# Attention units: the products with the values of one unit back ahead of the current unit's transposes

## The reference

```python
def masked_softmax(logits, mask):
    logits = jnp.where(mask, logits, -jnp.inf)
    m = jnp.max(logits, axis=-1, keepdims=True)
    p = jnp.exp(logits - m)
    return p / jnp.maximum(jnp.sum(p, axis=-1, keepdims=True), 1e-30)

# eight heads: o = g0 * o_cmp + g1 * o_slc + g2 * o_win
p = masked_softmax(jnp.einsum('bghqd,bgkd->bghqk', q_b, k_b) * scale, mask)
...
# four stick-breaking heads
z = jnp.einsum('bhqd,bhkd->bhqk', q_b, kf) * scale
log_1m = jnp.where(strict, log_beta - z, 0.0)
excl = lax.cumsum(log_1m, axis=3, reverse=True) - log_1m
a = jnp.where(strict, jnp.exp(log_beta + excl), 0.0)
...
# four forgetting heads: logits + c[query] - c[key], then masked_softmax
# memory: four heads, softmax over all 256 memory tokens
```

## Time and profile before

| | before |
|---|---|
| median of 3 runs | 1633.99 us (1633.25 to 1635.56) |
| the profiled execution's own time | 1634.43 us |
| its span | 1632.7 us |
| TensorE busy | 1587.6 us (97%) |
| VectorE busy | 1167.6 us (72%) |
| ScalarE busy | 816.3 us (50%) |
| GpSimd busy | 83.5 us (5%) |
| DMA | 293.67 MB, mean 180 GB/s |
| mean granted TensorE clock | 0.997 of full speed |

### The profile page before, as it was taken

How to read it: one execution, slowest core, us unless ns; L and a number is a source line. 1 busy time by engine, 2 the same in 40 slices (tenths; PEclk the granted TensorE clock), 3 DMA queues, 4 the chain that set the end, 5 groups by cost and what they waited for, 6 DMA issues and landing times.

```text
span 1632.7 us, 35998 instructions
## 1 busy us (share of the span) xinstructions
PE 1587.6 (97%) x12358; PEld 1474.2 (90%) x12358; DVE 1167.6 (72%) x1780; ACT 816.3 (50%) x1343; POOL 83.5 (5%) x89
## 2 busy tenths in 40 slices
PE   8999899999999989999999999999999999999998
PEld 7987789999897879999989888889999999999997
DVE  5774789988987478888867454568777678676744
ACT  5555666653456576654545222235555355555533
POOL 3000001110400000110000000000000000000000
PEclk9999999999999999999999999999999999999999
DMA  8440435458764135447925543348555765455551
GB/s 343 169 143 11 158 130 177 170 192 278 268 225 151 56 118 177 167 168 270 344 93 181 168 155 129 130 161 315 192 182 180 250 222 184 168 180 180 181 185 46
DMA packets 81164, 293.67 MB, mean 180 GB/s; under 512 B 9152, under 2 KB 10688, under 8 KB 80320
## 3 DMA queue, kind: packets, MB, share of 16 engines
q1 hardware_dynamic: 78912, 283.31, 49.8%
q10 hardware_dynamic: 2176, 9.31, 1.5%
HBM read 291.53 MB, written 1.05 MB: 179 GB/s over the span
## 4 chain that ended last, share of the span: by engine, by line
PE 73%; DVE 14%; ACT 6%; issue 4%; DVEq 1%; ACTq 1%; DMA 0%; POOL 0%; SPq 0%; POOLq 0%
PE projs L1632 34%; PE accs L1632 33%; PE ob L1632 5%; DVE WL L951 4%; ACT WH L472 3%; DVE mk L1314 2%; DVE cv L1323 2%; DVE cv L1321 1%; ACT FH L536 1%; DVE rstd L1082 1%; PE projs L1878 1%; DVE ring L968 1%; ACT scr L642 1%; DVE prod L1330 0%; DVE scr L1158 0%
## 5 line engine op out<-in xcount | busy, mean ns | idle before, releaser
L951 DVE TENSOR_TENSOR WL<-ring,WH 128x1024 fp32r<-128x1024 f32 x427 | 531.5, 1246 | 269.5 <-ACT WH L472 267.9
L472 ACT ACTIVATE WH<-ring 128x1024 fp32r (+1 forms) x419 | 441.6, 1057 | 545.2 <-PE projs L1632 270.5
L1632 PE MATMUL projs<-AH,WH 128*128 128x256 f32 (+2 forms) x2120 | 539.9, 292 | 12.3 <-ACT WH L472 4.1
L1632 PE MATMUL projs<-AL,WH 128*128 128x256 f32 (+2 forms) x2120 | 530.9, 287 | 0.3
L1632 PEld LDWEIGHTS projs<-AH,WH 128*128 128x128 f32 x2120 | 399.4, 189 | 28.8 <-DVE mk L1314 14.1
L1632 PEld LDWEIGHTS projs<-AL,WH 128*128 128x128 f32 x2120 | 401.2, 190 | 5.6 <-DVE AL L1109 1.7
L1632 PE MATMUL projs<-AH,WL 128*128 128x256 f32 (+2 forms) x2192 | 315.2, 285 | 0.4 <-DVE WL L951 0.4
L1632 PEld LDWEIGHTS projs<-AH,WL 128*128 128x128 f32 x2192 | 285.3, 189 | 7.6 <-DVE WL L951 3.1
L1632 PE MATMUL accs<-FH,WH 128*128 (+1 forms) x768 | 190.7, 285 | 2.0 <-ACT WH L472 2.0
L1632 PE MATMUL accs<-FL,WH 128*128 (+1 forms) x768 | 189.6, 279 | 0.0
L1632 PEld LDWEIGHTS accs<-FH,WH 128*128 128x128 f32 x768 | 144.0, 187 | 3.3 <-issue 3.3
(11 more groups left out here) (264 smaller groups left out, 1887.5 us busy)
## 6 DMA issues: line engine op xcount, KB each, us to landing
ring<-in_stream SPq DMA_DIRECT2D x532, 512.0 KB, 3.4
W1v<-in_w ACTq DMA_DIRECT2D x2, 1024.0 KB, 7.4
W1k<-in_w ACTq DMA_DIRECT2D x2, 1024.0 KB, 10.5
D<-in_decay ACTq DMA_DIRECT2D x4, 512.0 KB, 5.4
x<-in_xT SPq DMA_DIRECT2D x2, 512.0 KB, 4.9
memT<-in_memT SPq DMA_DIRECT2D x1, 1024.0 KB, 11.2
ctxT<-in_ctxT ACTq DMA_DIRECT2D x1, 1024.0 KB, 9.0
out_y<-ybuf SPq DMA_DIRECT2D x8, 128.0 KB, 2.0
```

Source lines behind the costliest of these rows:

```text
L472: A(WH[:, s, :], ring[:, r % RING, :], ACT.Copy).then_inc(wh_ready, 1)
L951: V.tensor_tensor(WL[:, s, :], ring[:, r % RING, :], WH[:, s, :].bitcast(F32), ALU.subtract).then_inc(consumed, 1)
L1632: return T.matmul(out, lhsT, rhs, start=start, stop=stop, skip_group_check=True)
```

## The change

In the loop over the units, TensorE issues `values(v - 1)` ahead of `turn(v)` instead of behind it. The other engines' streams are the same, row by row.

```diff
--- before.py
+++ after.py
@@ -1906,9 +1906,9 @@
                 for v in range(U):
                     if v + 2 < U:
                         scores(v + 2)
-                    turn(v)
                     if v:
                         values(v - 1)
+                    turn(v)
                 values(U - 1)
                 n["u"] += U
                 n["soft"] = softs[-1]
```

## The result

| | before | changed |
|---|---|---|
| median (6 runs each) | 1633.62 us (1632.96 to 1635.56) | 1640.36 us (1640.17 to 1640.60) |
| the profiled execution's own time | 1634.43 us | 1640.17 us |
| its span | 1632.7 us | 1638.5 us |
| TensorE busy | 1587.6 us | 1588.3 us |
| mean granted TensorE clock | 0.997 | 0.997 |

The account below looks back on a forecast made before the run. TensorE's own work, 73% of the span, was taken as the bound. Memory units 2.68, stick units +0.63 and -0.54, soft units 0 gave +2.77 us: 1637.20 for the profiled execution, 1636.8 for the median; range 1634.9 to 1639.2.

Parts of the forecast that it names:

- TensorE's scores run ahead by about 1.0 us by unit 7: Soft and forget units: values fill old waits, gaining 0.6 at turn(1) and some 0.2 each at turn(3) and turn(5).
- The copy of unit 8 starts at 539.68, not 539.65: Layer 1, soft units: the lead is spent again, unit 10's activations keep their time; 0 per layer, gain 0.9 to loss 0.4.
- or if turn(10) itself moves: Sign that the forecast is wrong: the start of stick unit 10's turn was expected to stay in place.
- Stick units: Layer 1: values(9) fits the idle gap, but turn(11) must wait for unit 10's copy and values(10): +0.63 us.
- I take -0.54: Layer 0's stick units: values(9) fills the idle stretch, the clock holds and turn(11) comes 0.54 us earlier; +0.55 if it falls.
- 1.61 us: Layer 0's stick units: cost given to the clock's fall, from turn(10) 3.27 against 2.18 and values(9) 1.32 against 0.80.
- rival (a): Nothing won back in layer 0: the clock falls there also, or usually did not before; 3.86 us, 1637.9, chance 0.28.
- turn(1) comes at 596.33: Memory units: turn(1) waits for the first copy and values(0), +1.34 us in each layer, 2.68 in all; bounds 1.2 and 1.5.
- Rival (b): The clock falls in the memory units because of TensorE's new idle times there: 1.6 us more, 1638.4, chance 0.12.

Follow-up runs that it names:

- units 1 to 7 alone: Kernel before with the new order in iterations 1 to 7 only, the old one from 8 on: 1636.28 us against 1634.33, ratio 1.0011.
- unit 8 alone: Kernel before with the new order in iteration 8 only, values(7) ahead of turn(8): 1635.80 us against 1634.33, ratio 1.0011.
- unit 11 alone: Kernel before with the new order in iteration 11 only, values(10) ahead of turn(11): 1635.95 us, ratio 1.0014.
- filled kernel: Changed kernel with four matmuls of a constant ahead of each values of the memory units: 1640.50 us against 1634.28 for the kernel before, ratio 1.0037.
- unit 10 alone: Kernel before with the new order in iteration 10 only, values(9) ahead of turn(10): 1633.14 us against 1634.28; repeated, 1633.68 against 1634.65.

## Why the prediction was wrong

Forecast for the profiled execution was +2.77 us; it became +5.74, and +6.74 between the medians. By the steps of the prediction:

1. **"TensorE's scores run ahead by about 1.0 us by unit 7": failed.** The first 0.6, at turn(1), came (scores(4) 0.62 earlier). The 0.2 each at turn(3) and turn(5) were eaten as they came: the lead of scores(5) to scores(8) is 0.47, 0.51, 0.35 and 0.39, then it shrinks to 0.25 at scores(9) and to 0.05 at scores(10). The reason lies in TensorE's own stream. Two iterations without a compressed product, with no wait in them, TensorE's timeline; before (v = 6):

```profile
530.20 0.38 PE L1632 MATMUL accs<-mqkb,identb 128*128 128x128 bf16 x4
530.42 0.82 PE L1878 MATMUL projs<-const,scr 128*128 128x128 f32 x6
531.17 0.87 PE L1632 MATMUL ob<-PT,Vt 128*64 128x256 f32 x8
531.97 0.71 PE L1632 MATMUL accs<-P 64*128 64x128 f32 x6
```

and the changed kernel (v = 2; its v = 6 takes 1.92):

```profile
518.04 0.40 PE L1632 MATMUL accs<-mqkb,identb 128*128 128x128 bf16 x4
518.37 0.87 PE L1632 MATMUL ob<-PT,Vt 128*64 128x256 f32 x8
519.17 0.88 PE L1878 MATMUL projs<-const,scr 128*128 128x128 f32 x6
519.97 0.71 PE L1632 MATMUL accs<-P 64*128 64x128 f32 x6
```

   From the mask to the next scores it is 1.77 us before and 1.93 now, with the same instructions: 0.16 more for the order. I had charged no price for an order of matmuls; several units of it eat the lead. Why the hand-overs cost more in this order (0.33 instead of 0.22 behind the mask, 0.80 instead of 0.75 behind the transposes) was not tried.

2. **"The copy of unit 8 starts at 539.68, not 539.65": failed.** In the same count it started about 0.75 later (543.51 - 507.30 = 36.21, before 539.65 - 504.19 = 35.46). So my own sign of being wrong came, "or if turn(10) itself moves". The delay follows from step 1 and from something that I overlooked. I followed turn(7), its copy, values(7) and turn(8), and left out that ScalarE does exps(9) between the copies of units 7 and 8. The run with units 1 to 7 alone shows this way by itself (0.37 in layer 1), the run with unit 8 alone the other (0.56). Together they cost 0.65 and 0.81 us at turn(10), where I had put 0 with an upper bound of 0.4 per layer. This is 1.46 of the 2.97 us that my sum lacked.

3. **Stick units, "+0.63": right.** Measured 0.62 in layer 1, and 0.61 with unit 11 alone. The move at unit 10 costs nothing, as forecast.

4. **"I take -0.54" for layer 0: the number came (0.55), the reason did not hold.** The fall was absent in this execution, but values(9) in the gap does not exclude it: it came in 5 of 16 layers with it. The "1.61 us" that I gave as the cost of the fall was also misread: it is how much longer turn(10) and values(9) took, but in layer 1 turn(11) had to wait 0.37 us for its cut behind them, so that the fall cost 4.59 - 3.42 = 1.17. The page of the Trainium skill that I had set against this step ("TensorE: Matmul & The Clock Gate", "What's actually happening") says that what watches the engine's activity is not reset when a kernel starts, so that the point of a change varies. The three traces of the changed kernel agree: beside the fall at the start that all of them have, they have one at 205, at 147 and at 550 us. I had given that possibility, rival (a), 0.28, and put only 1637.9 on it.

5. **Memory units, "turn(1) comes at 596.33", 2 x 1.34: right in mechanism, small by 0.15 each.** I took the starts of the values' pairs as the price of what follows them (4 x 0.215 = 0.86). The transposes behind them start only after 1.01 us, and so does their first weight load (the row at 600.85, with 0.39 us of idle PEld, "issue", ahead of it). Some 0.05 of the 0.15 could have been read before: the last of the eight starts 0.70 behind the first in both kernels (before, values(1): 597.29 to 597.99), and 0.215 more makes 0.91. The other 0.1 is the same error as in step 1: a hand-over between two kinds of matmuls that no row of before showed in this order. Why it takes longer is not shown. The whole makes 0.30 over both layers, and 1.5 was my upper bound.

6. **Rival (b) happened in this execution**: a fall behind the memory units, +1.52 (priced 1.6). Its reason stays open. One of eight such places had it in the new order and none of fourteen in the old, which is too little to say that the short waits bring it, and the filled kernel, without them, had its fall elsewhere. The same page of the Trainium skill ("A second HAM failure mode: psum-queue depth-cycling") would have the clock swing in the waits between groups of matmuls; inside the memory units no trace shows that, the granted clock is 1.00 there in all thirteen.

Together: 1.46 from steps 1 and 2, 0.30 from step 5, 1.52 from step 6, and -0.27 in the rest make 3.01, against 2.98 between forecast (2.77) and span (5.75). Steps 1, 2 and 5 with the rest would have given 2.77 + 1.76 - 0.27 = 4.26 us, or 1638.3, still inside my range; the fall carried the time out of it. The range was too narrow since all bounds on the soft units were taken from a lead that I assumed, and since I counted a fall that leaves one place as gone, not as free to come in another. Between the medians another 1.0 us lies. The six times of before spread over 2.6 us, and its profiled execution is 0.8 above its median; the changed ones lie within 0.5, and its profiled execution is 0.2 below. By the priced falls (1.63 at the start, 1.17 at turn(10)) the kernel before without any would take 1631.6, and the changed one without its two (1.63, 1.52) 1637.0: the order by itself costs about 5.4 us, worked out and not measured. Against 1632.12, the one execution whose trace has no fall at the places counted above or at 822 us (unit 10 alone, a move that costs nothing), it would be 4.9.

## What to carry to other kernels

On an engine whose items keep their order, an item moved ahead of the start of a chain (transposes, copy, values) is added to that chain unless the chain has slack of its own; follow the delay also through the in-order streams of the engines in between, with all that stands between two items on them. Move only where the item behind waits for something that comes later than the end of all that is moved: at unit 10 that held, and it cost nothing; in units 1 to 7, at 8 and 11 and in the memory units it did not. And where a trace shows a fall of the clock, price the change without it, and keep the fall as a separate case in both kernels.

## What the runs showed of the hardware that was not expected

- The same matmuls cost about 0.15 us more per unit in the order values, transposes, scores than in transposes, values, scores, with no wait in between (1.92 to 1.94 against 1.77 to 1.79 us, three iterations of layer 1 each).
- Transposes that follow the 64-column products of a memory unit start 1.01 us after the first of them and 0.31 after the last, though the pairs of those products start 0.21 to 0.27 us apart.
- A wait of TensorE of 1.75 us, with 0.8 us of work behind it, was followed by a fall of the clock to 0.50 in some executions and not in others of the same kernel; behind 2.18 us it fell in layer 0 and not in layer 1 of the same execution (kernel before).
- A fall costs 1.17 us where the work behind it waits for another engine anyway, and up to 1.7 where it does not. One at 822 us cost 0.2.
